# Hybrid RWKV-7 and differential-attention layer: chain steps placed in the inversion's insertions, attention maps combined before they are normalised

## The reference, cut to what matters

```python
hn = rms_norm(h, pre_norm_w)             # h: 16 meta tokens + 512 tokens, 2048 wide
proj = hn @ w_in                         # 2048 x 8320
y_r = rwkv7_branch(...) * silu(g_r)      # 16 heads of 64
y_d = diff_attn_branch(...) * silu(g_d)  # 8 heads, two 64-wide maps each, values 128 wide
y = concat([y_r, y_d]) @ w_out
h = h + rms_norm(y, post_norm_w)

# rwkv7: one step of the recurrence, per head
sa = einsum('vk,k->v', S, -kk_t)
S = S * w_t + sa b_t^T + v_t k_t^T
y = S r_t

# differential attention, per head and block of 128 queries
p = softmax(mask(q k^T / 8))             # two maps, c = 0, 1
attn = p[0] - lam * p[1]
o = attn @ v
o = rms_norm(o, subln_w, 1e-5) * (1 - lambda_init)
```

## Time and profile before

| | |
|---|---|
| median of 3 runs | 1413.96 us (1411.19 to 1417.52) |
| the profiled execution's own time | 1415.31 us |
| its span | 1413.5 us |
| mean granted TensorE clock | 0.988 of 2.4 GHz |
| busy: PE, PEld, DVE, ACT, POOL | 94%, 81%, 50%, 48%, 34% |
| one RWKV iteration in the steady part | about 86 us |
| one attention iteration in the steady part | about 57 us |

### The profile page before, as it was taken

How to read it: one execution, slowest core, us unless ns; L and a number is a source line. 1 busy time by engine, 2 the same in 40 slices (tenths; PEclk the granted TensorE clock), 3 DMA queues, 4 the chain that set the end, 5 groups by cost and what they waited for, 6 DMA issues and landing times.

```text
span 1413.5 us, 23929 instructions
## 1 busy us (share of the span) xinstructions
PE 1334.1 (94%) x9393; PEld 1138.2 (81%) x9393; DVE 708.4 (50%) x1557; ACT 674.6 (48%) x1550; POOL 479.7 (34%) x362
## 2 busy tenths in 40 slices
PE   3999999999999999999999989999999999989997
PEld 3988788787888878888788878888888887768885
DVE  5345756757566575765755433443444434430013
ACT  4445655556565555655555544344453444422321
POOL 3342223232232323223232333434334343324443
PEclk9999999999999999999999999999999999989999
DMA  6221111211111111111111222222222222225433
GB/s 208 71 82 54 53 51 46 59 46 47 55 53 55 46 46 55 53 55 46 53 49 58 76 60 61 75 75 75 70 78 77 68 78 73 60 82 191 117 94 142
DMA packets 151264, 102.24 MB, mean 72 GB/s; under 512 B 6398, under 2 KB 140640, under 8 KB 149600
## 3 DMA queue, kind: packets, MB, share of 16 engines
q1 hardware_dynamic: 151152, 100.71, 23.9%
HBM read 96.49 MB, written 4.19 MB: 71 GB/s over the span
## 4 chain that ended last, share of the span: by engine, by line
PE 80%; DVE 9%; ACT 5%; issue 3%; POOL 2%; DMA 0%; DVEq 0%; ACTq 0%; SPq 0%
PE tile L536 46%; PE tile L796 2%; PE tile L797 2%; PE tile L798 2%; PE ma L762 2%; PE ma L668 2%; PE ma L635 1%; PE ma L675 1%; ACT w_hi L874 1%; PE ma L656 1%; PE mb L777 1%; POOL arena L1181 1%; PE mb L712 1%; PE mb L779 1%; PE ma L796 1%
## 5 line engine op out<-in xcount | busy, mean ns | idle before, releaser
L1166 POOL TENSOR_TENSOR w_lo<-w_raw,w_hi 128x512 fp32r<-128x512 f32 x324 | 430.0, 1328 | 856.1 <-ACT w_hi L874 856.1
L536 PE MATMUL tile<-hn_hi,w_hi 128*128 128x264 f32 (+1 forms) x1696 | 445.6, 326 | 0.2
L536 PE MATMUL tile<-hn_hi,w_lo 128*128 128x264 f32 (+1 forms) x1696 | 438.5, 322 | 2.2 <-ACT arena L1051 2.2
L536 PE MATMUL tile<-hn_lo,w_hi 128*128 128x264 f32 (+1 forms) x1696 | 438.2, 321 | 0.0
L874 ACT CAST w_hi<-w_raw 128x512 fp32r<-128x512 f32 x324 | 200.4, 619 | 368.2 <-PE tile L536 256.1
L536 PEld LDWEIGHTS tile<-hn_hi,w_hi 128*128 128x128 f32 x1696 | 276.8, 190 | 29.2 <-issue 10.2
L536 PEld LDWEIGHTS tile<-hn_hi,w_lo 128*128 128x128 f32 x1696 | 276.4, 190 | 18.6 <-ACT arena L1051 3.6
L536 PEld LDWEIGHTS tile<-hn_lo,w_hi 128*128 128x128 f32 x1696 | 276.0, 190 | 11.4 <-issue 2.2
L1470 DVE TENSOR_TENSOR arena<-ma,c 128x384 f16<-128x384 f32 x120 | 66.9, 557 | 53.6 <-PE ma L656 51.9
L1048 ACT ACTIVATE arena<-ma 128x384 f16<-128x384 f32 x120 | 58.9, 491 | 45.5 <-PE ma L668 43.9
L1181 POOL TENSOR_TENSOR arena<-arena,power 128x10 f32<-128x10 f32 (+3 forms) x28 | 44.4, 1587 | 57.3 <-DVE arena L1368 37.1
(11 more groups left out here) (262 smaller groups left out, 2099.6 us busy)
## 6 DMA issues: line engine op xcount, KB each, us to landing
w_raw<-w_in SPq DMA_DIRECT2D x260, 256.0 KB, 2.8
w_raw<-w_out SPq DMA_DIRECT2D x64, 256.0 KB, 3.0
big<-x SPq DMA_DIRECT2D x4, 1024.0 KB, 8.1
arena<-x SPq DMA_DIRECT2D x4, 1024.0 KB, 8.7
out<-big SPq DMA_DIRECT2D x3, 1024.0 KB, 3.9
arena<-post_norm_w SPq DMA_DIRECT2D x1, 1024.0 KB, 4.9
out<-big SPq DMA_DIRECT2D x2, 512.0 KB, 3.2
arena<-table_rope SPq DMA_DIRECT2D x2, 264.0 KB, 2.9
```

Of the source, the lines that this page charges most:

```text
L536: last = mm(o[:, at:at + n], w[:, slot, cols], t[:, kt, tok:tok + n], start=(kt == 0 and w is w_hi and t is hn_hi), stop=(kt == KT - 1 and ...
L1166: T(w_lo[:, slot, :], w_raw[:, slot, :], w_hi[:, slot, :].bitcast(F32), ALU.subtract).then_inc(s("lo_done"), 1)
```

## The change

The chain's steps move half an inversion step earlier (`CHAIN_FROM` 4.7 to 4.203), so that each falls due 0.003 of a step behind an inversion step and is put into the same insertion, behind it. The copies of DVE and ACT for the chain get a common offset (`CHAIN_COPY` 0.55) in place of 0.3, and ACT's scaling of the state goes to 0.75. Two places of the GroupNorm and two of the operand products move. In the attention, the two maps are combined with the exponentials as they are, map 0 minus lam sum0 / sum1 times map 1 (`at_share`), and the division by sum0 is done in the copy of the output from PSUM. `lam` is kept negated in a new [P, 1] tensor.

```diff
--- before.py
+++ after.py
@@ -150,6 +150,7 @@
         gate_sub = sb("gate_sub", [P, 1])
         half_decay = sb("half_decay", [P, 1])
         lam = sb("lam", [P, 1])
+        minus_lam = sb("minus_lam", [P, 1])
         power = sb("power", [P, 16])
         lora = sb("lora", [P, TPX])
 
@@ -243,6 +244,7 @@
         at_neg = carve("attn", "at_neg", 2)
         at_sum = carve("attn", "at_sum", 2)
         at_inv = carve("attn", "at_inv", 2)
+        at_share = carve("attn", "at_share", 1)
         at_var = carve("attn", "at_var", 4)
         at_pow = carve("attn", "at_pow", 4)
 
@@ -286,10 +288,11 @@
 
 
         INV_AT, INV_SPAN, INV_STEPS = 0.6, 21.1, 15.19
-        CHAIN_FROM, CHAIN_STEP = 4.7, 1.0
+        CHAIN_FROM, CHAIN_STEP = 4.203, 1.0
+        CHAIN_COPY = 0.55
         TURN_AT, LEVEL_AT, LEVEL_STEP = 2.2, 3.2, 2.0
         LATE_AT, LATE_STEP = 0.85, 0.7
-        GN_AT, GN_SPREAD, GN_TURN, GN_DVE = 18.5, 7.1, 8.8, (9.5, 11.7, 14.5)
+        GN_AT, GN_SPREAD, GN_TURN, GN_DVE = 18.5, 7.1, 9.5, (10.25, 12.2, 14.5)
         GATE_AT = 36
         ROPE_AT = (26, 39.5)
         LORA_LAG = 4
@@ -297,7 +300,7 @@
         NORM_AT, LORA_AT, KK_AT = 34.6, 36.4, 39.4
         SCAN_AT, KK_DVE, E_AT = (38.55, 39.15), 40.8, 40.9
         B_AT, K_AT = 42.4, 45.3
-        PADS_AT = (46.2, 46.75, 48.98, 51.25)
+        PADS_AT = (46.2, 48.1, 49.2, 51.25)
         AR_AT, RKP_AT, BONUS_AT, BONUS_DVE = (52.85, 55.0), 57.1, 58.3, 59.6
         MIDDLE_AT, LAST_AT = (3.1, 3.6), (24.1, 24.6)
         TILE_AT = {"rwkv": 16.1, "attn": 15.5, None: 15.5}
@@ -1055,7 +1058,7 @@
                 for c in range(GC):
                     ch = g * GC + c
                     home = suv[:, chunk_home(i, ch, late), :]
-                    yield chain_at(g, 3 * c + 0.3, late, work)
+                    yield chain_at(g, 3 * c + 0.75, late, work)
                     if 0 < ch < SC:
                         act.wait_ge(s("s_taken"), states_so_far(i, ch - 1, late))
                         if ch == 1:
@@ -1063,7 +1066,7 @@
                         for h, rows in enumerate(halves):
                             last = A(state0[rows, :], home[rows, rows], ACT.Copy, scale=w_end_of(i, late)[rows, ch:ch + 1])
                         last.then_inc(s("s_scaled"), 1)
-                    yield chain_at(g, 3 * c + 1.3, late, work)
+                    yield chain_at(g, 3 * c + 1 + CHAIN_COPY, late, work)
                     if 0 < ch < SC:
                         act.wait_ge(s("s_scaled"), kept_so_far(i, ch, late))
                     act.wait_ge(s("u_done"), chunks_so_far(i, ch, late))
@@ -1285,7 +1288,7 @@
                 dve.wait_ge(s("lam_dots"), n + 1)
             dve.wait_ge(s("lam_exp"), 1)
             steps(TT(lam[:], lam_s[:, 2:3], lam_s[:, 3:4], ALU.subtract))
-            steps(TS(lam[:], lam[:], LAM0, None, ALU.add))
+            steps(TS(minus_lam[:], lam[:], LAM0, -1.0, ALU.add, ALU.mult))
             for v in (xk, xv, xr, lora):
                 V.memset(v[:, 0:PAD], 0.0)
             V.memset(lora[:, TP:TPX], 0.0)
@@ -1489,16 +1492,16 @@
                     ch = g * GC + c
                     m = chunks_so_far(i, ch, late)
                     home = suv[:, chunk_home(i, ch, late), :]
-                    yield chain_at(g, 3 * c + 0.3, late, work)
+                    yield chain_at(g, 3 * c + CHAIN_COPY, late, work)
                     dve.wait_ge(s("g_done"), m)
                     V.tensor_copy(g_sb, mb[:, 0:P]).then_inc(s("g_taken"), 1)
-                    yield chain_at(g, 3 * c + 1.3, late, work)
+                    yield chain_at(g, 3 * c + 1 + CHAIN_COPY, late, work)
                     dve.wait_ge(s("u_done"), m)
                     if 0 < ch < SC:
                         dve.wait_ge(s("s_scaled"), kept_so_far(i, ch, late))
                     V.tensor_copy(home[top, top], mb[top, top]).then_inc(s("u_taken"), 1)
                     if ch < SC:
-                        yield chain_at(g, 3 * c + 2.3, late, work)
+                        yield chain_at(g, 3 * c + 2 + CHAIN_COPY, late, work)
                         dve.wait_ge(s("s_done"), states_so_far(i, ch, late))
                         if ch == 0:
                             dve.wait_ge(s("ends_made"), i - late)
@@ -1562,13 +1565,13 @@
                     yield base + 5
                     dve.wait_ge(s("exp_made"), c * 2)
                     steps(V.reciprocal(at_inv, at_sum))
-                    steps(TT(at_inv[:, 1:2], at_inv[:, 1:2], lam[:], ALU.mult))
-                    steps(TS(prob[1][:, 0:width], prob[1][:, 0:width], at_inv[:, 1:2], None, ALU.mult))
-                    STT(prob[0][:, 0:width], prob[0][:, 0:width], at_inv[:, 0:1], prob[1][:, 0:width], ALU.mult,
-                        ALU.subtract).then_inc(s("combined"), 1)
+                    steps(STT(at_share, at_sum[:, 0:1], at_inv[:, 1:2], minus_lam[:], ALU.mult, ALU.mult))
+                    STT(prob[0][:, 0:width], prob[1][:, 0:width], at_share, prob[0][:, 0:width], ALU.mult,
+                        ALU.add).then_inc(s("combined"), 1)
                     yield base + 11
                     dve.wait_ge(s("pv_done"), c)
-                    V.tensor_copy(o_sb[:, qi * P:(qi + 1) * P], mb[:, 0:P]).then_inc(s("o_taken"), 1)
+                    TS(o_sb[:, qi * P:(qi + 1) * P], mb[:, 0:P], at_inv[:, 0:1], None,
+                       ALU.mult).then_inc(s("o_taken"), 1)
                 at = attn_at(gn, 3)
                 yield at + 12.5
                 dve.wait_ge(s("o_squared"), n * 4)
```

## The result

The changed kernel takes **1430.17 us** (median; 1429.82 to 1431.58), the kernel before 1412.58 beside it on the same chip: 1.0124 of the time before, interval 1.0099 to 1.0149. It is slower by 17.6 us. The forecast was no change, 1414, with a range to 1423: the kernel is slower than any time in that range. The kernel before has a lower granted clock in many of its runs than the kernel after (0.988 in the profiled one, against 0.993), so the clock hides some of the loss.

What follows compares the result with a forecast made beforehand. The prediction took PE as the bound, with 80% of the chain of waits. Its terms, -7.8 + 9.7 + 7.0 + 2.8 - 5.8 - 5.9 = 0.0 us, gave 1414 us, no change, range 1403 to 1423.

Steps and rivals of the forecast that it cites:

- Part 1: PE: chain steps sharing an insertion with f16 inversion steps save 0.055 us each, 142 times: 7.8 us saved.
- part 2: ACT: copy of y now precedes the last level's x and xt, so x is late: 23 x 0.42 = 9.7 us lost.
- part 3: DVE, group 2: with the second k-half product moved, g's and the state copy come late: 7 x 1.0 = 7.0 us lost.
- Part 4: ACT, level 2 of group 1 and level 3 of group 2: copies behind the cast 0.17 later, 2.8 us lost.
- part 5: GroupNorm transposes on PE: the 0.84 us wait for ACT goes in seven iterations, 5.8 us saved.
- Part 6: Attention: transposes wait less for DVE's combined map, 4.45 us, plus 1.5 from the clock; together 5.9 us saved.
- The comparison with the transposes of V: PE: three f16 matmuls followed by two fp32 records cost 0.41 us joint, 0.46 to 0.47 apart: 0.055 saved.
- The rival that the joints give nothing: PE insertions: joint ones save nothing and the new waits stay whole, 1422 us; chance 0.13.
- the slack of 0.06 from the joint: PE's residual after the y copy: due 1.61 us after L668, less 0.06 for the joint; 0.4 us lost.
- the first wait: Group 2: PE wants g's copy at 594.4, DVE makes it at about 595.7; PE waits over 1 us.
- the longer wait at L715: End of group 2's stretch: DVE's state copy ends near 599.5, making PE some 1.0 us late.

Runs made afterwards that it cites:

- experiment 8: Changed kernel with PE's chain steps one insertion point later, in insertions of their own, DVE and ACT orders kept: 1426.44 us, ratio 1.0074.
- experiment 4: Changed kernel with ACT's copy of y moved behind x and xt of the last level: 1419.33 us, ratio 1.0041.
- experiment 5: Changed kernel with the operand products (PADS) back at their old places: 1424.26 us, ratio 1.0058.
- experiment 6: Changed kernel with the y copy behind x and xt and the operand products at their old places: 1413.15 us, ratio 1.0001.
- experiment 2: Kernel before with the change's attention part and its GroupNorm places only: 1400.28 us, ratio 0.9899.
- experiment 1: Kernel before with the change's attention part only: 1405.48 us, ratio 0.9936.
- experiment 11: ACT's due copies ahead of its cast: changed kernel with y copy and operand products mended, 1413.74 us; kernel before with attention and GroupNorm parts, 1406.49.
- experiment 12: Due copies ahead of ACT's cast, DVE's masks and operand products later: 1391.01 us with attention and GroupNorm parts, 1397.93 with joint insertions added.

## Why the prediction was wrong

| part | forecast, us | measured, us | by |
|---|---|---|---|
| 1 joint insertions | -7.8 | 0 | prices above, experiment 8 |
| 2 y copy | +9.7 | +10.8 | experiment 4 |
| 3 DVE stretch | +7.0 | +5.9 | experiment 5 |
| 4 other copies, and whatever else the joints bring | +2.8 | +12.9 | experiment 6 against 2 |
| 5 GroupNorm | -5.8 | -5.2 | experiment 2 |
| 6 attention | -5.9 | -9.5 | experiment 1 |
| sum | 0.0 | +14.9 | |

From 1415.0, the kernel before beside these experiments, the measured column gives 1429.9 and the kernel after 1430.2. Most rows are steps from one kernel to the next, so their sum has to come near the total; what experiment 6 tests is that parts 2 and 3 add.

**Part 1 is a step that failed.** The price of a joint was read from the only one in the trace, with fp32 transposes behind f16, and carried over to products. "One fp32 product (two records) alone puts on 0.22" was right. The comparison with the transposes of V was not; they are another kind of fp32 work, and the same place with u's product costs 0.46 to 0.47 and not 0.41. That the weight loads differ too, 141 ns for 190, is one row that would have warned. The rival that the joints give nothing was there, with 0.13, and named the doubt itself ("its fp32 matmuls are transposes"). By itself it gives 1422.

The Trainium skill (TensorE: Matmul & The Clock Gate, What happens when you issue a matmul, Step-by-step) says that weights are loaded ahead of the matmuls in flight if the row groups do not conflict or the load goes to the background weight buffer. In so far as the prediction took from it that a change of operand kind costs nothing, the joint prices here agree, within 0.015 us.

**Part 4 is the step with the largest error.** (Its own product, 16 x 0.17, is 2.7.) The mechanism, a copy released by a unit's end with the chain's product ahead of it, was right, and it was counted at two places of an iteration where there were more: level 1 of group 0 has it too (0.43 at 552.58, none before), the copies of V made PE wait 7.0 instead of 4.0, and L725 waits 5.0 for the xt copy where the main stream had waited 2.2. The sentence that failed stands in the sum: "PE's other waits (the 0.8 us at the start of group 2, the V copies) hang on nothing that moves." The V copies hang on ACT's queue, in which the chain's copies had moved. Of the 12.9, PE's rows show 8.6: 4.7 at L659, 3.1 at L678, 2.8 at L725, 0.1 at L671, less 2.1 at L715, which waits less for the state copy. For the rest there are only the weight loads, here of experiment 6's kernel:

```profile
PEld mb L725 <- issue: 2.7, 15, 0.2
...
PEld mb L720 <- issue: 1.3, 7, 0.2
```

Neither row exists in experiment 2's kernel; they are chain steps whose loads come 0.18 us late. Their 4.0 us are of the size of the missing 4.3. That they are it was not tested alone.

**Parts 2, 3 and 5 came within 1.1 us**, part 2 by its mechanism, the other two in part by luck. In part 2 the slack of 0.06 from the joint did not exist, so 0.46 and not 0.42. In part 3 the order and the first wait were right, but the sum took the delay from the state copy at the end of the stretch, and there the longer wait at L715 did not come (0.5 us in the whole kernel for 2.6 before). In part 5 the wait went as forecast, but was worth 0.55 us in six of the seven iterations and not 0.84, 4.2 together; the profiles have another 2.2 behind the first score, where it changes nothing (experiment 2).

**Part 6 was too small** by 3.6 us, in both of its terms. For the waits it had 4.45; at the same clock of 0.991 experiment 1 gives 6.2 to 6.5. Only waits of PE's matmul row were counted, six of 17; the five steady heads, which have none there, gained 5 x 0.37 = 1.9, which is about the difference. For the clock it had 1.5, one stretch at 1.2 GHz; by difference, an estimate, the medians hold about 3, since the kernel before is at 0.988 in most of its runs. The last iteration's parts came as worked out: the third block's combination at 0.64 and no fall of the clock behind it.

The Trainium skill (SBUF — State Buffer, Who interferes with whom) says that the order of issue decides which of the two engines blocks on the shared pair of ports. The trace agrees: with 0.10 us of lead DVE took 0.64 and POOL 1.67, against a mean of 1.31 over the span; with POOL ahead by 0.31 DVE took 1.51.

**The direction.** The losses but for PADS have one pattern. In this kernel the copies' order is set by places in common with PE's steps; the change moved PE's steps ahead of work that they do not need and the copies ahead of work that PE does need. The one reward for that was the joint, and it is zero.

## What to carry to other kernels

A discount read from a neighbourhood of two operations holds only for that pair: before it is multiplied by 142, take the price apart and joint from the same kind of operation, and compare the weight loads. When work moves on one engine, list every wait on every queue that it is moved past, those called independent as well, and read the waits of the weight loads beside those of the matmuls. A copy that stands behind a cast pays for the cast's release; taking it ahead moves what the cast triggers (here a subtraction on a third engine), in every stage where the edit applies. Compare an edit stage by stage, and with the granted clock beside the time: experiment 11 gains in one stage and loses more in the next, and single runs of one kernel differ by up to 14 us with the clock.

## What the runs showed that was not expected

- Weight loads of 128x128 have three prices in these insertions: f16 96 to 99 ns, the fp32 transposes of V and of the combined map 140 to 142, the chain's fp32 products 188 to 192. The order of kinds beside each other does not change what an insertion costs, by 0.015 us.
- An edit of where ACT casts (experiment 11) reaches PE through an engine that it does not name: POOL's subtraction, 1.26 us, stretched two DVE products from 1.5 to 2.57, and in iteration 9 it stood ahead of the GroupNorm's power, for a wait of 2.8. The first did not make the kernel slower by itself: its iterations were 0.4 us shorter.
- The granted clock fell near short waits, and not each time: at the end of two of the seven waits of 2.4 us at L671 (experiment 11), and up to 2.9 us behind three of the seven of 0.6 at L725 (experiment 12). That these waits are the reason is not shown. A fall for 3.4 us lengthened an iteration by 1.4 to 1.6 us.
- Edits that are worth nothing or less each (the cast ahead: +6.2; DVE's places: +0.7) are together worth -9.3 us: 1400.28 to 1391.01.
